# Two weight loads of the second feed-forward wait for the first w products of the gated delta rule

## The chip, the cores and the metric

One core of a Trainium2 chip. The metric is the device time of one execution in microseconds, the median of several runs. Times inside the kernel are counted from the start of the span of one profiled execution.

## What is computed

A decoder trunk of two layers on 256 tokens of width 1024, all in f32. Each layer adds a half feed-forward, a mixer and another half feed-forward:

```
for l in range(DEPTH):
    x = x + 0.5 * swiglu(rms_norm(x, norm_w[l, 0]), ...)
    h = rms_norm(x, norm_w[l, 1])
    x = x + (mixer_mla_gdn(h, ...) if l % 2 == 0 else mixer_spatial_gating(h, ...))
    x = x + 0.5 * swiglu(rms_norm(x, norm_w[l, 2]), ...)
```

The mixer of layer 0 has eight attention heads and eight heads of a gated delta rule. The latter works in chunks of 64 tokens: it solves a unit triangular system of 64 rows for each chunk and head, then goes through the four chunks in a recurrence:

```
sol = lax.linalg.triangular_solve(a, rhs, left_side=True, lower=True, unit_diagonal=True)
u, w = sol[..., :dv], sol[..., dv:]
def step(state, xs):
    v_new = u_i - w_i @ state
    o_i = qd_i @ state + a_i @ v_new
    state = state * exp(gl_i) + kt_i^T @ v_new
```

## The kernel before

**Weights in units.** All large weights are cut into units of at most 128x2048 elements (1 MB) and stream through a ring of four slots. For unit j, SyncE loads it into `raw` slot j % 4 (`load_unit`), ACT rounds it to `whi` (`hi`, L469), and VectorE subtracts to get `wlo` (`lo`, L892; for two units GpSimd does it, L439). TensorE multiplies with `whi` and `wlo`, which stands in for full f32. The load of unit j waits until the `wlo` of unit j - 4 is made, since that is the last reader of the `raw` slot: `lo_done(j - SLOTS)`.

**Order.** The kernel is written engine by engine; each engine's program is a fixed list, with semaphores between. SyncE's list is the loads in the order of use, then the stores of the result. A wait in it holds all loads behind it.

**Around the change.** Layer 0's mixer uses units `u_ab` to `u_ab + 15`; the last four are the output projection. The second feed-forward (of the same layer) uses the 33 units from `u_ffn[1]` on. Its first unit (gate) takes the slot of `u_ab + 12`, its second (up) that of `u_ab + 13`; the `wlo` of those two is made by GpSimd (`POOL_LO`) and counted by `pool_lo_ready`. Its third unit takes the slot of `u_ab + 14`, whose `wlo` VectorE makes after the recurrence.

**What TensorE does there.** After attention it builds the inverse of the triangular matrices by merging: five rounds (n = 0 to 4), each with the products m1, d and dt for two halves t of the tokens, by `quadrants` (L1710); ACT and VectorE move the sums out of PSUM between them. Then `AT_sums` (L1697), the w products (L1826), the transposes of q (L1835), the products u of the inverse with v (L1848), and the recurrence: for n = 0 to 3 the products with the state (L1861, L1865, not for n = 0), the state's update (L1873, not for n = 3) and the outputs (L1879). `w_sums` is counted up after the w products of t = 0 and again after those of t = 1; ACT copies w out then (L762). The output projection begins behind the recurrence (L1367).

A matmul of 64x64 in f32 leaves two matmul records and two weight-load records in the trace.

Of the kernel before, what the change touches and what calls it, by code (L numbers as in the profile page):

```python
# [73 lines left out]
def build_trunk(nc, x, positions, norm_w, w_gate, w_up, w_down, ab_in, q_norm, w_q_b, kv_norm, w_kv_b,  # L74
# [65 lines left out]
    for j, (_, _, pieces) in enumerate(units):  # L140
        per_slot[j % SLOTS] += len(pieces) if j else 0
        arrivals.append(per_slot[j % SLOTS])
# [4 lines left out]
    with ctx:  # L147
# [5 lines left out]
        def S(name):  # L153
            if name not in sems:
                sems[name] = ctx.enter_context(nc.semaphore(name))
            return sems[name]
# [126 lines left out]
        def unit_view(ring, j, kt, width):  # L283
            return ring[:, j % SLOTS, 0:kt * width].rearrange("p (k n) -> p k n", n=width)
# [10 lines left out]
        def lo_done(j):  # L295

            if j in POOL_LO:
                return S("pool_lo_ready"), POOL_LO.index(j) + 1
            return S("lo_ready"), j + 1 - sum(1 for i in POOL_LO if i < j)
# [16 lines left out]
        @block.sync  # L316
        def _(sp_):

            def load(dst, src, name):
                sp_.dma_start(dst, src).then_inc(S(name), 16)  # L320

            def load_first(i):
                load(unit_view(raw, 0, 8, 256)[:, 2 * i:2 * i + 2, :], units[0][2][0][1][:, 2 * i:2 * i + 2, :],
                     f"first_loaded{i}")

            for n in range(2):
                c = slice(512 * n, 512 * n + 512)
                for t in range(NT):
                    load(X[:, t, c], x[0, t * P:(t + 1) * P, c], f"x_loaded{t}{n}")
                load_first(n)  # L330
            for i in (2, 3):
                load_first(i)

            def load_unit(j):

                kt, width, pieces = units[j]
                if j >= SLOTS:
                    sp_.wait_ge(*lo_done(j - SLOTS))
                for c0, src in pieces:
                    dst = unit_view(raw, j, kt, width)[:, :, c0:c0 + src.shape[2]]  # L340
                    sp_.dma_start(dst, src).then_inc(S(f"raw_loaded{j % SLOTS}"), 16)

            def ffn_loads(base):
                for j in range(base, base + 33):
                    if j:
                        load_unit(j)
                    if j == 2:
                        load(C[:, P:n_const], const_dram[:, P:n_const], "const_loaded")

            ffn_loads(u_ffn[0])  # L350
            if stop_after == "ffn0":
                pass
            else:
                for j in range(u_ab, u_ab + 16):
                    load_unit(j)
            if stop_after not in ("ffn0", "ab"):
                ffn_loads(u_ffn[1])
                ffn_loads(u_ffn[2])
                for j in range(u_sg, u_sg + 24):
                    load_unit(j)  # L360
                ffn_loads(u_ffn[3])

            n_x = {"ffn0": 1, "ab": 2}.get(stop_after, 6)
            for q, (t, n) in enumerate(QUARTERS):
                sp_.wait_ge(S("x_updated"), 4 * (n_x - 1) + q + 1)
                sp_.dma_start(out[0, t * P:(t + 1) * P, 512 * n:512 * n + 512], X[:, t, 512 * n:512 * n + 512]
                              ).then_inc(S("out_stored"), 16)
            sp_.wait_ge(S("out_stored"), 64)
# [1596 lines left out]
```

## Time and profile before

| what | us |
|---|---|
| median of 3 runs | 1101.32 (1099.79 to 1102.14) |
| the profiled execution | 1101.23 |
| its span | 1099.3 |
| TensorE busy | 1066.0 (97% of the span) |
| TensorE weight loads busy | 971.4 (88%) |
| VectorE busy | 641.6 (58%) |
| ACT busy | 514.7 (47%) |
| GpSimd busy | 45.0 (4%) |

A chain of waits follows back from the last instruction, at each step to what released it. In its rows "issue" is time in which the engine waited for nothing that the profile shows. Windows show each engine's busy time in a stretch, with the granted TensorE clock as a share of full speed and the DMA engines' busy share. The DMA view lists the packets of each queue in a stretch; the queue of kind "instruction" brings instructions to an engine, the one called "hardware_dynamic" the loads that SyncE issues.

### The profile page before, as it was taken

What the parts mean: (1) busy time and instruction counts of PE and PEld (TensorE: products, weight loads), DVE (VectorE), ACT (ScalarE), POOL (GpSimd) and SP (SyncE); (2) the same over time, 40 slices, a digit from 0 to 9 for tenths busy, and PEclk for the clock granted to TensorE, in tenths of its full rate; (3) what the DMA queues carried; (4) which work ended last, traced back from release to release, by engine and by line L of the source; (5) the groups of instructions that cost most, each with busy time, mean ns of one, the idle gap of its engine ahead of it and who ended that gap; (6) DMA issues with size and microseconds to landing.
All of it is one profiled execution on the core that took longest, in us unless ns stands there. A gap on an engine that the chain in (4) does not pass through costs nothing.

```text
span 1099.3 us, 18954 instructions
## 1 busy us (share of the span) xinstructions
PE 1066.0 (97%) x8393; PEld 971.4 (88%) x8393; DVE 641.6 (58%) x779; ACT 514.7 (47%) x619; POOL 45.0 (4%) x34
## 2 busy tenths in 40 slices
PE   7999999998968999999999999999999999999998
PEld 6999988997757899999889999888788889999986
DVE  5755543699752775555348555545755547655532
ACT  6644433684653454444335444335565436444430
POOL 1000000112160000000000000000100000000000
PEclk9999999999999999999999999999999999999999
DMA  9855556253020466655547655555555475655531
GB/s 308 273 181 188 190 191 179 87 192 115 2 76 7 154 195 189 192 192 186 182 130 230 191 180 182 180 190 171 163 176 198 154 230 171 186 183 190 192 114 39
DMA packets 127194, 184.88 MB, mean 168 GB/s; under 512 B 4205, under 2 KB 101722, under 8 KB 126986
## 3 DMA queue, kind: packets, MB, share of 16 engines
q1 hardware_dynamic: 126368, 181.85, 50.9%
q0 software_dynamic: 448, 1.71, 0.5%
q8 instruction: 66, 1.08, 0.4%
q10 hardware_dynamic: 298, 0.12, 0.0%
q14 instruction: 14, 0.11, 0.0%
HBM read 182.62 MB, written 1.05 MB: 167 GB/s over the span
## 4 chain that ended last, share of the span: by engine, by line
PE 88%; DVE 5%; ACT 3%; issue 2%; DMA 1%; POOLq 0%; SPq 0%; POOL 0%; DVEq 0%; ACTq 0%
PE banks L1326 19%; PE banks L1327 19%; PE banks L1328 19%; PE banks L1367 7%; PE banks L1371 7%; PE banks L1368 7%; PE banks L1710 2%; DVE arena L1059 1%; PE banks L1436 1%; PE banks L1438 1%; PE banks L1437 1%; DVE wlo L892 1%; DMA raw<-in_ffn_w_up 1%; ACT whi L469 1%; PE banks L1400 1%
## 5 line engine op out<-in xcount | busy, mean ns | idle before, releaser
L892 DVE TENSOR_TENSOR wlo<-raw,whi 128x2048 fp32r<-128x2048 f32 (+1 forms) x169 | 386.7, 2294 | 228.5 <-ACT whi L469 228.4
L469 ACT ACTIVATE whi<-raw 128x2048 fp32r<-128x2048 f32 (+1 forms) x171 | 324.0, 1907 | 384.4 <-PE banks L1328 241.4
L1326 PE MATMUL banks<-xTh,whi 128*128 128x256 f32 x1408 | 396.8, 282 | 1.6 <-DVE wlo L1014 0.9
L1327 PE MATMUL banks<-xTl,whi 128*128 128x256 f32 x1408 | 395.8, 281 | 0.0
L1328 PE MATMUL banks<-xTh,wlo 128*128 128x256 f32 x1408 | 395.7, 281 | 0.0
L1326 PEld LDWEIGHTS banks<-xTh,whi 128*128 128x128 f32 x1408 | 265.5, 189 | 2.6 <-issue 1.2
L1327 PEld LDWEIGHTS banks<-xTl,whi 128*128 128x128 f32 x1408 | 265.6, 189 | 0.0
L1328 PEld LDWEIGHTS banks<-xTh,wlo 128*128 128x128 f32 x1408 | 265.5, 189 | 0.0
L1367 PE MATMUL banks<-whi,hTh 128*128 128x512 f32 x352 | 139.4, 396 | 0.0
L1368 PE MATMUL banks<-wlo,hTh 128*128 128x512 f32 x352 | 139.0, 395 | 0.0
L1371 PE MATMUL banks<-whi,hTl 128*128 128x512 f32 x352 | 110.6, 395 | 0.0
L1371 PEld LDWEIGHTS banks<-whi,hTl 128*128 128x128 f32 x352 | 66.0, 187 | 16.1
L1367 PEld LDWEIGHTS banks<-whi,hTh 128*128 128x128 f32 x352 | 66.0, 187 | 15.9
L1368 PEld LDWEIGHTS banks<-wlo,hTh 128*128 128x128 f32 x352 | 66.0, 187 | 15.8
L1326 PE MATMUL banks<-whi,xTh 128*128 128x512 f32 (+1 forms) x160 | 64.0, 400 | 0.0
L1327 PE MATMUL banks<-wlo,xTh 128*128 128x512 f32 (+1 forms) x160 | 62.7, 392 | 0.0
L1328 PE MATMUL banks<-whi,xTl 128*128 128x512 f32 (+1 forms) x160 | 62.6, 391 | 0.0
L927 DVE TENSOR_TENSOR arena<-banks,arena 128x512 f32<-128x512 f32 x44 | 30.4, 691 | 53.5 <-PE banks L1328 53.5
L918 DVE TENSOR_TENSOR arena<-banks,arena 128x512 f32<-128x512 f32 x44 | 30.4, 690 | 26.9 <-PE banks L1328 26.9
L1326 PE MATMUL banks<-whi,hTh 128*128 128x512 f32 (+1 forms) x108 | 43.6, 404 | 0.0
L1328 PE MATMUL banks<-whi,hTl 128*128 128x512 f32 (+1 forms) x108 | 42.2, 390 | 0.0
L1327 PE MATMUL banks<-wlo,hTh 128*128 128x512 f32 (+1 forms) x108 | 42.1, 390 | 0.0
(241 smaller groups left out, 976.6 us busy)
## 6 DMA issues: line engine op xcount, KB each, us to landing
raw<-in_ffn_w_up SPq DMA_DIRECT2D x44, 1024.0 KB, 5.4
raw<-in_ffn_w_down SPq DMA_DIRECT2D x44, 1024.0 KB, 4.9
raw<-in_ffn_w_gate SPq DMA_DIRECT2D x43, 1024.0 KB, 5.4
raw<-in_sg_w_in SPq DMA_DIRECT2D x16, 1024.0 KB, 5.5
raw<-in_ab_w_in SPq DMA_DIRECT2D x8, 1024.0 KB, 5.2
raw<-in_sg_w_out SPq DMA_DIRECT2D x8, 1024.0 KB, 5.3
raw<-in_ab_w_out SPq DMA_DIRECT2D x4, 1024.0 KB, 4.9
raw<-in_ab_w_in SPq DMA_DIRECT2D x2, 832.0 KB, 4.4
```

Of the source, the lines that this page charges most:

```text
L469: A(whi[:, j % SLOTS, 0:kt * width], raw[:, j % SLOTS, 0:kt * width], ACT.Copy).then_inc(S("hi_ready"), 1)
L892: TT(wlo[:, j % SLOTS, 0:n], raw[:, j % SLOTS, 0:n], whi[:, j % SLOTS, 0:n].bitcast(f32), ALU.subtract).then_inc(S("lo_ready"), 1)
L918: TT(gate[:, c % 2, :].rearrange("p (b n) -> p b n", n=SEQ), B[PAIR_BANK[c][0]][:].rearrange("p (b n) -> p b n", n=SEQ), bc(r_row.unsqueez ...
L927: TT(prod[:, c % 2, :], B[PAIR_BANK[c][1]][:], gate[:, c % 2, :], ALU.mult).then_inc(S("prod_ready"), 1)
L1059: ins = STT(y, src[:, 0:SEQ - back], w, y, ALU.mult, ALU.add)
L1326: mm(out_ap, lh, rh, start=first, stop=False)
L1327: mm(out_ap, lh, rl, start=False, stop=False)
L1328: return mm(out_ap, ll, rh, start=False, stop=last)
L1367: mm(o, hTh[:, kk, tok], wh[:, k, c], start=kk == 0, stop=False)
L1368: mm(o, hTh[:, kk, tok], wl[:, k, c], start=False, stop=False)
L1371: last = mm(o, hTl[:, kk, tok], wh[:, k, c], start=False, stop=False)
L1710: last = mm(banks[HC[r ^ s], pair[s], 64 * i:64 * i + 64], left, right, start=True, stop=True)
```

## The change

One line: SyncE waits until `w_sums` is at least 1 before it issues the loads of the second feed-forward.

```
@@ -354,6 +354,7 @@
                 for j in range(u_ab, u_ab + 16):
                     load_unit(j)
             if stop_after not in ("ffn0", "ab"):
+                sp_.wait_ge(S("w_sums"), 1)
                 ffn_loads(u_ffn[1])
                 ffn_loads(u_ffn[2])
                 for j in range(u_sg, u_sg + 24):
```

SyncE's list, where the output projection's four loads end and the second feed-forward's begin; `raw` is the ring, the brackets name the semaphores that a DMA waits for:

```order
 L341 DMA raw<-in_ab_w_out 128x2x1024 [waits lo_ready] x4
-L341 DMA raw<-in_ffn_w_gate 128x8x256 [waits pool_lo_ready]
+L341 DMA raw<-in_ffn_w_gate 128x8x256 [waits pool_lo_ready,w_sums]
 L341 DMA raw<-in_ffn_w_up 128x8x256 [waits pool_lo_ready]
 L341 DMA raw<-in_ffn_w_gate 128x8x256 [waits lo_ready]
```

The gate unit has a second semaphore to wait for; the up unit stands behind it and its own wait is unchanged.

TensorE's list from the w products to the second step of the recurrence, in the kernel before; `arena` holds the working matrices, `banks` is PSUM:

```order
1905 L1826 MATMUL banks<-arena 64x64 [waits dt_merged,kbe_ready]
1906 L1826 MATMUL banks<-arena 64x64 x15
1907 L1826 MATMUL banks<-arena 64x64 [waits dt_merged]
...
1911 L1848 MATMUL banks<-arena 64x64 [waits vb_ready,at_ready]
1912 L1848 MATMUL banks<-arena 64x64 x31
1913 L1873 MATMUL banks<-arena 64x64 [waits v_new_even,kt_ready,v_new_odd,qdT_out,w_ready]
1914 L1873 MATMUL banks<-arena 64x64 x7
1915 L1879 MATMUL banks<-arena 64x64 x8
1916 L1861 MATMUL banks<-arena 64x64 [waits state_ready]
```

Nothing moved on TensorE: its list after is the same. `w_sums` reaches 1 behind the row 1906; the two loads, which stood free of it, are now issued from there on.

## Rows read from the trace of the kernel before

**Rows 1.** Page: engines (busy, share, count), instruction queue (packets, MB), chain by engine.

```profile
PE 1066.0 (97%) x8393; PEld 971.4 (88%) x8393; DVE 641.6 (58%) x779; ACT 514.7 (47%) x619; POOL 45.0 (4%) x34
...
q8 instruction: 66, 1.08, 0.4%
...
PE 88%; DVE 5%; ACT 3%; issue 2%; DMA 1%; POOLq 0%; SPq 0%; POOL 0%; DVEq 0%; ACTq 0%
```

**Rows 2.** Timeline of SyncE's queue, 320 to 366 us: start, duration, line, tile.

```profile
320.99 0.37 SPq L341 DMA_DIRECT2D raw<-in_ffn_w_gate  x1
325.48 0.37 SPq L341 DMA_DIRECT2D raw<-in_ffn_w_up  x1
365.46 0.37 SPq L341 DMA_DIRECT2D raw<-in_ffn_w_gate  x1
```

**Rows 3.** Chain in order of time, 315 to 360 us: start, duration, what.

```profile
321.70 2.15 PE banks L1710 x125
323.85 4.50 issue
328.35 3.48 PE banks L1710 x95
331.82 0.60 issue
332.42 2.20 PE banks L1710 x127
334.62 1.25 issue
335.86 2.13 PE banks L1710 x124
337.99 1.51 issue
339.51 0.39 PE banks L1710 x10
...
343.14 0.51 PE banks L1697 x10
...
347.13 0.86 PE banks L1848 x21
...
350.06 0.06 PE banks L1861
...
352.60 0.06 PE banks L1861
```

**Rows 4.** DMA view, 321 to 325.75 us: all packets.

```profile
DMA packets 1035, 1.05 MB, mean 220 GB/s; under 512 B 13, under 2 KB 1035, under 8 KB 1035
```

**Rows 5.** DMA view, 325.75 to 326 us: instruction queue.

```profile
q8 instruction: 1, 0.02, 27.3%
```

**Rows 6.** DMA view, 344.5 to 344.75 us: instruction queue.

```profile
q8 instruction: 1, 0.02, 23.6%
```

**Rows 7.** Windows, TensorE: stretch, length, busy (count), clock, DMA share, GB/s.

```profile
308.00:310.00 2.00, 2.00 (x49) 0.50 0.00 0
...
328.00:330.00 2.00, 1.65 (x60) 0.51 1.08 375
330.00:332.00 2.00, 1.82 (x75) 0.64 0.04 12
```

**Rows 8.** Timeline of ACT: w copied out, and first feed-forward unit rounded.

```profile
344.25 1.22 ACT L762 ACTIVATE arena<-banks 128x256 f32<-128x256 f32 x4
...
365.27 1.95 ACT L469 ACTIVATE whi<-raw 128x2048 fp32r<-128x2048 f32 x1
```

**Rows 9.** DMA view, 324.75 to 325 us: the queue of SyncE's loads.

```profile
q1 hardware_dynamic: 96, 0.10, 110.4%
```

**Rows 10.** DMA view, 349.5 to 349.75 us: instruction queue.

```profile
q8 instruction: 1, 0.02, 32.4%
```

**Rows 11.** Timeline of TensorE, 302 to 308 us, idle before in brackets.

```profile
307.19 0.53 PE L1740 MATMUL banks<-C,arena 128*128 128x128 f32 x3 [2.64 <-ACT arena L698]
```

More of the change, by code:

```diff
@@ L356, in _ @@
             if stop_after not in ("ffn0", "ab"):
+                sp_.wait_ge(S("w_sums"), 1)
                 ffn_loads(u_ffn[1])
```

## The prediction

> **What bounds the kernel now.** Begin with the chain that ended last: TensorE holds 88% of it, everything else is small, 2% is "issue", time in which an engine waited for nothing that the profile shows [rows 1]. Time can come back only where TensorE stands still. The change moves two weight loads, so the next view is SyncE's issues around them: the gate unit at 320.99, the up unit at 325.48, and no further load before 365.46 [rows 2]. Only these two move. The third load after them waits for a `wlo` subtraction that VectorE does after the recurrence, as before.
>
> Third, the chain piece by piece over 320 to 353 us [rows 3]. Here TensorE runs the merges of the inverse, 64x64 matmuls, in pieces of some 127 records (a f32 matmul leaves two), and between pieces stands "issue": 4.50, 0.60, 1.25 and 1.51 us. These are no waits for ACT or VectorE. The page has a DMA queue of kind "instruction" with 66 packets and 1.08 MB [rows 1]: 16 KB a packet. A piece of 127 records is 127 weight loads and 127 matmuls, 254 instructions; the page counts 8393 of each, and 16786 over 66 packets are 254 again [rows 1]. So each piece is one packet, and "issue" is TensorE waiting for its next packet of instructions. With no load about, TensorE resumes at 332.42, 335.86, 339.51 and 343.14 [rows 3]. Those periods are 3.44, 3.65 and 3.63, mean 3.57 us, of which the matmuls fill 2.1 to 2.3; there the fetch is the bound.
>
> The 4.50 us stall stands under the first load. That load's 1035 packets are all that the DMA engines moved from 321 to 325.75 [rows 4]; the instruction packet comes only in the quarter us behind them [rows 5], at 325.79 in the answer's slices, and TensorE resumes 2.56 us later, at 328.35. In the quiet the packet of 344.74 [rows 6] comes 1.6 us after TensorE resumed at 343.14; here it came 4.1 us after 321.70. It waited for one load's share of its DMA engine. After the idle time the granted clock is 0.51 and then 0.64 on the mean of 2 us each [rows 7], which is the lower level, 1.2 GHz, for 2 x (0.49 + 0.36) x 2 = 3.4 us: the piece at 328.35 takes 3.48 us where others take 2.13 to 2.20.
>
> **What the merges give back.** From 321.70 to 332.42 are two pieces, 10.72 us. Without loads they should take two quiet periods, 2 x 3.57 = 7.14. Gain: 3.58 us. It is all on the path: the pieces before and after are TensorE or its fetch. The stall doesn't vanish to zero; what is late next is the ordinary fetch, and that is in the 3.57. Bounds from the rows: two periods of 3.44 give 3.84, two of 3.65 give 3.42.
>
> **What the wait adds.** SyncE has only the two loads and those behind them queued at this point; nothing else waits for SyncE. `w_sums` 1 is reached when half of the w products are made: ACT, which waits for the same count, starts at 344.25 [rows 8]. (All times stay on the clock of before; the shift of 3.6 us moves both sides alike.) GpSimd's subtractions, the other condition, were over when the up unit was issued at 325.48, so both loads are issued one behind the other at about 344.3 and 344.7. The first issue of before had its data moving from 322.0 and done by 325.8, 1.0 and 4.8 us after it. So load 1 moves from 345.3 to 349.05; load 2 follows without a gap, 64 packets of 1 KB on each of 16 engines, at 96 packets a quarter us over all engines, the rate in the middle of the first load [rows 9], 2.7 us, to about 351.8. Their data is wanted by ACT at 365.27 [rows 8]: 13 us of cover. If that cover went, each us late would cost a us; it does not go.
>
> **What the loads now lie over.** The recurrence: the v products and the first two of its steps, matmuls of the same small kind. It uses instructions slower, since it waits for VectorE in each step of some 2.5 us (350.06 to 352.60) [rows 3], and shows no fetch stall now. Fetches in it come at 344.74 [rows 6], for the boundary that is passed at 347.13, and at 349.59 [rows 10], for the next. That boundary: 21 records from 347.13, six batches of 16, and with the extra waits of the steps about 8 records of the third state product, which starts around 352.5 [rows 3]. Between packet and resuming stood 2.56 us in the merges, and at most 2.39 from 344.74 to 347.13; with 2.5, the packet at 349.59 lets TensorE go on at 352.1: 0.4 us to spare. But at 349.05 the fetch's engine has gone over to load 2. If the fetch waits for the share in progress, as it did for the first load, it comes at 351.8, TensorE resumes at 354.3, and 354.3 - 352.5 = 1.8 us is lost, on the path, since the steps are a chain. The bounds: nothing, if it slips in between the loads; 2.5 if load 2 is spread like a lone one.
>
> By the Trainium skill, "DMA: Bandwidth & Descriptors", section "Queues, rings and completion order", an engine changes rows after a packet of some 9 to 17 descriptors, at most 64. The 4.1 us above agree with the ceiling of 64, a whole share, not with the typical figure; by that figure nothing would be lost in the recurrence.
>
> **Sum.** -3.58 + 1.8 = -1.8 us. The profiled execution took 1101.23 us (span 1099.3), the median is 1101.32: the forecast is 1099.5 us, a change of 0.16%. A measurement of this kernel tells about 0.2%, 2.2 us, from no change.
>
> **Rivals.**
>
> The fetch slips in (gain whole). The request of the packet at 349.59 is made when the recurrence's first step is released at about 348.5, before load 1 ends at 349.05. If it is served in the change between the two loads, nothing is lost: 1101.3 - 3.6 = 1097.7. For it: the rows show a fetch behind one load, never behind two. Against: in the kernel before the packet came 1.1 us after that release, which is half a us too late for the change. The typical figure of the Trainium skill's DMA page would give this case too.
>
> The stall in the recurrence also costs the clock. After an idle of 2.64 us [rows 11] the clock was 0.50 [rows 7], after stalls of up to 1.51 us it stayed full. The new stall, 1.8 us, stands between. At the lower level for 3.4 us the dense merges lost 3.48 - 2.13 = 1.35 us; the same here gives -1.8 + 1.35 = -0.4: 1100.9.
>
> The loads hit one fetch earlier (the slower case). The fetch at 344.74 has 0.5 us before the first data at 345.3. Its place is fixed by count of instructions, the load's by `w_sums`. If it comes behind load 1 instead, at 349.1, TensorE resumes at 351.6 instead of 347.1: 4.5 lost, and the clock as in the merges 1.35, so -3.58 + 5.85 = +2.3: 1103.6. It decides from half a us of slip; both sides hang on TensorE's own place, which speaks against it.
>
> The change does nothing. The Trainium skill, "Runtime: NRT & Kernel Launch", section "Instruction fetch mechanics", has blocks of 16 KiB, as the packets here, and calls their cost mostly hidden; by it no load could slow TensorE through its fetch, and the time would stay. As a mechanism of this kernel: the 4.50 us would be something that comes at this point of the merges whatever is loaded. Against it stand the four stalls between pieces of equal length. Result 1101.3.
>
> **How the numbers follow.** Forecast with the stall in the recurrence, 0.46; whole gain 0.27; stall with the lower clock 0.13; no change 0.06; slower case 0.07; 0.01 left. The range holds the first four with their bounds: low 1101.3 - 3.84 - 0.7 for scatter = 1096.8, high 1101.7 (no change and 0.4, the scatter of the runs shown); outside are the slower case and tails. Faster than 1099.1: the whole gain (0.25) and that third of the forecast's spread in which the stall is under 1.3 us (0.15): 0.40. Slower 0.07. Within: 0.53. Both likely cases are gains; the question is only whether they pass 2.2 us.
>
> **What would show it.** In the chain after: periods of 3.4 to 3.7 us all through the merges, no clock under 1.00 there, w products begun 3.6 us sooner. Two loads issued half a us apart just at the w products. An "issue" of 1 to 2.5 us in the second or third step of the recurrence, behind an instruction packet that comes right after load 2. Wrong if the 4.50 us stays with no load about; if the recurrence shows no stall (then 1097.7); or if the stall stands in the v products (1103.6).

## The result: a gain in the merges, and more than that lost in the recurrence

The changed kernel takes 1104.02 us (median of 9 runs, 1100.52 to 1108.06), the kernel before 1101.32 (9 runs). The ratio is 1.0026, 95% interval 1.0015 to 1.0036: slower by a quarter of a percent. The forecast was 1099.5 within 1096.8 to 1101.7. A second set of 11 runs gave 1.0017 (1.0004 to 1.0029). The profiled execution of the changed kernel took 1104.02 us, its span is 1102.2.

Line numbers behind the added line are higher by one: L1711 is the merges' matmul, L1862 the state product, L1874 the state update, L1780 the transposes at which the output projection waits for VectorE.

The chain of the changed kernel in order of time, 312 to 372 us (start, duration, what):

```profile
322.43 2.15 PE banks L1711 x125
324.57 1.76 issue
326.33 2.18 PE banks L1711 x126
328.51 1.41 issue
329.92 2.20 PE banks L1711 x127
332.11 1.52 issue
...
340.64 0.51 PE banks L1698 x10
...
348.36 0.68 PE banks L1874 x16
...
350.12 1.97 issue
...
353.64 0.87 PE banks L1874 x16
...
357.69 1.94 PE banks L1880 x16
...
366.43 0.87 PE banks L1780 x8
```

The 4.50 us stall of [rows 3] is gone, the pieces run at 2.13 to 2.20 us, and from 322.43 to 340.64 the same work takes 18.21 us where it took 21.44: 3.23 us less. In the recurrence a new stall of 1.97 us stands within the third step's state product, and behind it everything takes longer: the state update 0.87 for 0.68, the last outputs 1.94 for 1.13 (the row of before reads 356.29 1.13).

SyncE's issues in the changed kernel, as [rows 2]:

```profile
341.75 0.37 SPq L341 DMA_DIRECT2D raw<-in_ffn_w_gate  x1
342.16 1.12 SPq L341 DMA_DIRECT2D raw<-in_ffn_w_up  x1
```

The DMA view from 349.25 to 349.5 us has the instruction packet among the last packets of the loads, and the one from 349.5 to 350.5 us shows that 14 packets were left:

```profile
q8 instruction: 1, 0.02, 26.2%
```

```profile
DMA packets 14, 0.01 MB, mean 11 GB/s; under 512 B 3, under 2 KB 14, under 8 KB 14
```

TensorE's windows in the changed kernel (stretch, length, busy and count, granted clock, DMA share, GB/s), as [rows 7]:

```profile
352.00:354.00 2.00, 1.90 (x35) 0.50 0.00 0
...
358.00:360.00 2.00, 2.00 (x17) 0.50 0.00 0
360.00:362.00 2.00, 2.00 (x6) 0.55 0.03 8
362.00:364.00 2.00, 2.00 (x11) 1.00 0.00 0
```

The clock is at its lower level from the end of the stall until near 361.8, some 10 us, where it had been full.

**The ledger.** The stretch from the second state update to the transposes measures what the stall costs: 351.15 to 363.29 in the kernel before, 12.14 us; 348.36 to 366.43 in the changed one, 18.07. Of the 5.93 us more, 1.97 are the stall; the 3.96 that are left are put down to the half clock: 3.04 of them up to the end of the last outputs, 0.92 in the projection behind them. The rest, at the marks above: +0.73 us up to 322.43 (the half clock after the idle of [rows 11] lasted longer in this execution; see the end), -3.23 in the merges, -0.29 from there to 348.36, +5.93, together +3.14 at the transposes; the span is 2.9 longer.

### The profile page after: what moved, and what is told of

Same layout as the page of the kernel before. It is cut to its first block, busy times and chain, and to the rows that moved or that the text cites. A ratio compares the mean times of both kernels' runs of the same rounds, so it can differ in the third digit from the quotient of the medians.

```text
span 1102.2 us, 18955 instructions
## 1 busy us (share of the span) xinstructions
PE 1072.3 (97%) x8393; PEld 977.4 (89%) x8393; DVE 641.6 (58%) x779; ACT 514.7 (47%) x619; POOL 45.4 (4%) x34
## 4 chain that ended last, share of the span: by engine, by line
PE 89%; DVE 5%; ACT 3%; issue 2%; DMA 1%; POOLq 0%; SPq 0%; POOL 0%; ACTq 0%; DVEq 0%
PE banks L1327 19%; PE banks L1329 19%; PE banks L1328 19%; PE banks L1368 8%; PE banks L1372 7%; PE banks L1369 7%; DVE arena L1060 1%; PE banks L1711 1%; PE banks L1437 1%; PE banks L1438 1%; PE banks L1439 1%; DVE wlo L893 1%; DMA raw<-in_ffn_w_up 1%; ACT whi L470 1%; PE banks L1401 1%
```

## Experiments

Theory from here on: the two loads cost time only by holding up a packet of TensorE's instructions; the stall that this makes is short, and the dear part is the half clock (the granted clock at 0.50) behind it. Rivals: the loads slow the recurrence or the clock in themselves; the later arrival of the data costs; the first profile was chance.

### The wait on the last outputs

```
-                sp_.wait_ge(S("w_sums"), 1)
+                sp_.wait_ge(S("o_sums"), 4)
```

> The same wait, but on the last outputs of the recurrence (o_sums 4): both loads are issued where TensorE begins the output projection with 512-column matmuls, which use few instructions per us. Theory (the loads cost time only by delaying TensorE's instruction packets; in the changed kernel that gave a 1.97 us stall in the recurrence, and the half clock behind it cost the rest): merges as in the changed kernel, no issue stall in the recurrence, clock 1.00 from the merges to the projection, loads landed before ACT wants them; time 1101.3 - 3.2 = 1098.1, ratio 0.997. Rival (the later landing or the longer wait itself costs): ratio 1.000 or more, with TensorE or ACT waiting on a load near 362 to 372 us. Rival (the recurrence is slowed by something else than the loads): the 2 us stall and the half clock stand in the recurrence as before.

Ratio 0.9964 (0.9952 to 0.9977), 1099.12 us. Because only 6 runs stood behind it, it was run again beside two later kernels:

> The kernel that waits for the last outputs once more, beside the two others of this job. Theory: ratio to before 0.9955 to 0.998, no issue stall and clock 1.00 from 325 us to the projection. Rival (its first figure of 0.9964 was luck of 6 runs): 0.999 or above.

Ratio 0.9985 (0.9976 to 0.9993), 1099.99 us: a smaller gain. The ratio lies just above the expected 0.9955 to 0.998 and below the rival's 0.999, and the interval reaches into both. Both intervals of this kernel lie below 1. The second profile's chain, with no issue of note in the recurrence:

```profile
349.43 0.68 PE banks L1874 x16
...
354.56 1.13 PE banks L1880 x16
...
361.56 1.09 PE banks L1780 x8
```

349.43 to 361.56 is 12.13 us, what the kernel before has. The loads were issued at 356.08 and 356.49 (first profile), ran from 357 to about 364 under the projection, and nobody waited for them. The gain of the merges stays in the main: from the resumption at 323.04 to that at 341.80 us the first profile has 18.76 us, the second 18.70 (323.02 to 341.72), where the kernel before has 21.44. So neither the wait nor the later arrival costs. This kernel is faster than the one before and, by intervals that do not meet, than the changed one. The expectation that the clock is full from 325 us on missed: in the second profile one piece of the merges ran at half clock:

```profile
325.17 2.03 issue
327.20 3.59 PE banks L1711 x126
...
331.00 2.19 PE banks L1711 x127
```

It cost next to nothing: 327.20 to 331.00 is 3.80 us, and the full-clock periods in the profiles of this kernel and of the changed one are 3.4 to 4.2 us. The issue of 1.4 us that follows a full-clock piece is used up by the slow one. This is why the half clock was cheap in the merges [rows 3, 7] and not in the recurrence.

### One load over the recurrence instead of two

```
+                if j == u_ffn[1] + 1:
+                    sp_.wait_ge(S("o_sums"), 4)
...
+                sp_.wait_ge(S("w_sums"), 1)
                 ffn_loads(u_ffn[1])
```

> Only the gate unit's load waits for w_sums 1, the up unit's waits for o_sums 4: one load lies over the recurrence instead of two. Theory (a packet of instructions waits for the share of the load in progress on its DMA engine; in the changed kernel it was the second load that held it): the load's data end about 3.8 us after they begin, near 346.6 us, before the packet's usual time of 346.8, so no stall beyond 0.3 us and the clock stays at 1.00: ratio 0.997. Rival (any load over the recurrence does it, by memory contention or by its placement): a stall of 1 us or more and the half clock remain, ratio 1.001 to 1.003.

Ratio 0.9983 (0.9972 to 0.9995), 1100.28 us. In the profile (span 1097.2) there is no stall in the recurrence and the clock there is 1.00, with the load's data moving at 248 GB/s under it:

```profile
344.00:348.00 4.00, 3.33 (x102) 1.00 0.75 248
```

So a load over the recurrence does not slow it by itself. The forecast of 0.997 lies just outside the interval; the runs spread over 4 us, and no profile shows whether some of them had a stall.

### Loads in pieces

Each of the two loads is issued as four DMAs of 256 KB, once where they stood before and once as in the change. (The counts that the readers wait for are raised to match, not shown.)

```
+                if j in CUT:
+                    for i in range(4):
+                        r = slice(2 * i, 2 * i + 2)
+                        sp_.dma_start(unit_view(raw, j, kt, width)[:, r, :], pieces[0][1][:, r, :]
+                                      ).then_inc(S(f"raw_loaded{j % SLOTS}"), 16)
+                    return
```

> The kernel before, with each of the two loads issued as four DMAs of 256 KB (two of the eight k-rows each). Nothing else moved. Theory A (the DMA engine turns to the instruction queue after the DMA in progress): the 4.50 us stall in the merges shrinks to about 4.50 - 3 x 0.7 = 2.4 us or less, and with it the half clock; ratio 0.997 to 0.999. Theory B (it turns to it only after all that was already handed to it): four DMAs issued one behind the other act as one, the stall stays at 4 to 4.5 us, ratio 1.000.

Ratio 0.9994 (0.9986 to 1.0003). The stall under the first load is 2.58 us, and a second of 2.44 comes under the other load:

```profile
325.47 2.58 issue
328.05 2.91 PE banks L1717 x126
330.96 2.44 issue
333.40 6.61 PE banks L1717 x235
340.01 0.49 issue
```

The stall is shorter than B asks and a little longer than A's 2.4, but the run doesn't tell A from B: TensorE came to this place 1.6 us later than in the kernel before (323.33 for 321.70), so its packet met the loads at another point. It does show the half clock again: 235 records took 6.61 us and 0.49 of issue, 7.10 for nearly two periods, about as fast as at full clock. The granted clock was 0.50 from 332 to 336 us.

> The changed kernel, with each of the two loads issued as four DMAs of 256 KB. Theory A of the run before (turn after the DMA in progress): the packet wanted near 347 us comes at most 0.7 us late, no stall in the recurrence beyond 0.3 us, clock 1.00: ratio 0.997. Theory B: the packet comes at the end of all eight, near 349.3 us, stall 1.5 to 2 us and half clock, ratio 1.001 to 1.004 as the changed kernel.

Ratio 1.0003 (0.9988 to 1.0019); inconclusive as a time. The 12 runs fall into two groups: four from 1098.55 to 1100.61 us with a mean granted clock of 0.994 to 0.997, and eight from 1102.73 to 1106.44 with 0.989 to 0.992. The profile (1105.09 us) is clear: a stall of 1.24 us and the half clock behind it, 349.84 to 367.41 or 17.57 us where 12.13 is normal.

```profile
349.84 0.68 PE banks L1881 x16
...
351.60 1.24 issue
...
367.41 0.87 PE banks L1787 x8
```

The instruction packet comes in the DMA view from 350.25 to 350.5 us, and 456 packets of the loads still follow from 350.5 to 353 us:

```profile
q8 instruction: 1, 0.02, 21.9%
```

```profile
DMA packets 456, 0.43 MB, mean 173 GB/s; under 512 B 33, under 2 KB 456, under 8 KB 456
```

It came 3.1 us behind the release of the first state update at 347.33, in the kernel before 0.9 us (348.65 to 349.59): 2.2 us late. A (at most 0.7 us) falls, and B (behind all eight) falls too.

### Stalls without any load

Here the loads wait for the last outputs, and VectorE does a reduction more ahead of the second state update; its result is used by nobody. The operand is X with 1024, 1536 or 2048 columns; the code is that of the 2048. TensorE's own idle time is shorter than the reduction, since it still computes outputs beside it: it is in the brackets of TensorE's rows below.

```
                 dve.wait_ge(S("s_sums"), n + 1)
+                if n == 1:
+                    link(nc.vector.tensor_reduce(rs_t[:, 31:32], X.rearrange("p t n -> p (t n)"), AX.X, ALU.max))
```

> The kernel of the run that waits for the last outputs (no load and no fetch stall in the recurrence), with one extra VectorE reduction of 128x1024 of X (its result is used by nobody) ahead of the second state update. TensorE then stands still about 1.1 us longer before the third step's state products, with no DMA about. It asks what an idle of that length costs by the clock. Theory (the half clock follows the idle time itself, whatever caused it, and decides between 1 and 2 us): clock stays 1.00, the time is that kernel's plus 1.1 us, ratio to before 0.9974. Rival (the half clock has another cause, the loads for one): the same here.

Ratio 0.9983 (0.9971 to 0.9996), 1099.93 us. The reduction took 1.23 us and left TensorE idle for 0.90, the clock stayed at 1.00, and the stretch is 13.39 us (352.20 to 365.59), 1.26 more than normal: the reduction and nothing else.

```profile
352.99 1.23 DVE small L1262
```

```profile
354.72 0.68 PE L1864 MATMUL banks<-arena 64*64 64x64 f32 x16 [0.90 <-DVE arena L1265]
```

The profiled execution is one of the four long ones of the 12 (1103.45 us; the other eight took 1099.09 to 1100.90). Its extra time lies ahead of the recurrence, where the granted clock was 0.58 from 316 to 320 and 0.56 from 320 to 324 us.

> As the run before, with a reduction of 128x2048: TensorE stands still about 2.2 us longer, as long as under the fetch stall of the changed kernel, but without loads and with its instructions there. Theory (idle time alone brings the half clock): windows from about 351 to 360 us show 0.50, and the time is the waiting kernel's plus 2.2 plus 2 to 4 us, ratio 1.000 to 1.002. Rival (it is the loads or the fetch that bring the half clock): clock 1.00, plus 2.2 us only, ratio 0.9984.

Ratio 1.0036 (1.0025 to 1.0047), 1106.16 us. The stretch is 349.77 to 369.29, 19.52 us: 7.39 more, of which 2.30 are the reduction and 5.1 are left for the clock. TensorE's idle time is 1.97 us.

```profile
350.56 2.30 DVE small L1262
...
369.29 0.87 PE banks L1782 x8
```

```profile
353.36 1.12 PE L1864 MATMUL banks<-arena 64*64 64x64 f32 x16 [1.97 <-DVE arena L1265]
```

The windows: half clock with no DMA about until 362 us, and up to near 366.

```profile
352.00:354.00 2.00, 0.64 (x12) 0.60 0.00 0
354.00:358.00 4.00, 4.00 (x72) 0.50 0.02 4
358.00:362.00 4.00, 3.84 (x42) 0.50 0.00 0
362.00:366.00 4.00, 4.00 (x11) 0.50 0.89 272
```

So idle time of that length, which is that of the changed kernel's stall, brings the half clock at this place with no load and no fetch in it. The theory holds; the size was above its upper bound of 1.002.

> As the 2.2 us stall in the recurrence, with a reduction of 128x1536, 1.75 us. No loads near. It asks where the clock turns. Theory (between 1.2 and 2.0 us of idle, by where it falls): some runs with half clock and some without, times spread over 5 us or more, ratio 0.999 to 1.003. Rival (a sharp bound at or above 2 us): all runs at that kernel's time plus 1.75, ratio 0.998, and a full clock in the profile.

Ratio 1.0025 (1.0010 to 1.0039), 1104.99 us, 6 runs from 1102.41 to 1106.06. The reduction took 1.76 us and left TensorE idle for 1.44; the stretch is 350.27 to 368.46, 18.19 us: 1.76 for the reduction and 4.30 left for the clock.

```profile
353.32 0.68 PE L1864 MATMUL banks<-arena 64*64 64x64 f32 x16 [1.44 <-DVE arena L1265]
```

The runs of the waiting kernel beside it are 1098.16 to 1101.79; with 1.76 added they would end at 1103.55, and four of the six lie above that. So the half clock comes in most runs; the two lowest, 1102.41 and 1103.39, may be runs without it. In the profiles of the recurrence TensorE kept the full clock behind an idle of 0.90 us and had the half clock behind every longer one: 1.24 (the loads in pieces), 1.44, 1.70 (the changed kernel again, below) and 1.97 us twice. Length alone is not the rule everywhere: in the merges the clock stayed full behind 1.76 us in several profiles, and 2.03 us of issue at the same place was followed by the half clock in the second profile of the waiting kernel and by the full one in this run's.

### The same reduction in the merges

```
                         dve.wait_ge(S("yt_sums"), 2 * (n - 1) + t + 1)
+                    if n == 2 and t == 0:
+                        link(nc.vector.tensor_reduce(rs_t[:, 31:32], X.rearrange("p t n -> p (t n)"), AX.X, ALU.max))
```

> The kernel that waits for the last outputs, with the extra reduction of 128x2048 (2.30 us) ahead of the third merge's m1 on VectorE, so that TensorE idles in the merges and not in the recurrence. Theory (the price of a stall is what its half clock meets: in the merges a piece of 127 records at half clock takes 3.3 us, no more than the 3.57 us that its next instructions take anyway, so the half clock is nearly free there): windows near 330 to 340 us show 0.50, pieces of 3.3 us with little issue between, and the time is that kernel's plus 1 to 2.5 us, where the same idle in the recurrence cost 7 to 8. Rival (a stall with half clock costs about the same wherever it stands): plus 6 us or more.

Ratio 0.9978 (0.9968 to 0.9988), 1099.01 us, against 0.9985 for the waiting kernel on the same chip: the 2.30 us of VectorE cost nothing. TensorE's timeline shows why:

```profile
323.01 2.15 PE L1713 MATMUL banks<-arena 64*64 64x64 f32 x127 [0.83 <-issue]
326.92 0.34 PE L1713 MATMUL banks<-arena 64*64 64x64 f32 x7 [1.76 <-issue]
327.42 1.98 PE L1713 MATMUL banks<-arena 64*64 64x64 f32 x119 [0.16 <-DVE arena L1232]
```

The reduction ran from 324.36 to 326.66 us, beside products that did not need it and then beside the 1.76 us in which TensorE waited for its next instructions anyway; the waiting kernel's first profile has the same 1.76 there. VectorE held TensorE up for 0.16 us. So the long idle that was expected never came, the clock stayed at 1.00, and the run does not test what such an idle costs in the merges. It shows that a late VectorE is free there. That half clock is cheap in the merges rests on the two profiles above, the second of the waiting kernel and that of the loads in pieces where they stood before.

### The changed kernel again

> The changed kernel once more, for a second profile and times on the same chip as the others. Theory: merges without the 4.50 us stall, a stall of 1.5 to 2.5 us in the recurrence, then half clock for 3 to 10 us; ratio 1.001 to 1.004. Rival (the first profile's half clock was chance): the stall, but full clock, ratio about 0.999.

Ratio 1.0017 (1.0004 to 1.0029), 1104.11 us. The stall is 1.70 us, the half clock lasts from near 352.8 to 363, the stretch is 18.37 us (348.13 to 366.50): 1.70 for the stall and 4.54 left for the clock. The instruction packet came between 349 and 349.25 us, with 22 packets of the loads left behind that. The first profile was no chance.

### The loads half way through the recurrence

```
-                sp_.wait_ge(S("w_sums"), 1)
+                sp_.wait_ge(S("v_sums"), 2)
```

> The wait on v_sums 2, one and a half steps into the recurrence: both loads move from about 348 to 354.6 us, past the fetch that the changed kernel hit and over the next one (before: 353.28, here 350.1). Theory (every fetch that falls under both loads comes at their end): its packet comes near 354.6 instead of 350.1, and TensorE stalls up to 3 us at the begin of the output projection, where the clock may fall too; ratio 0.998 to 1.002. Rival (only the recurrence is sensitive, the projection's long matmuls hide it): no stall, ratio 0.9965 as for the wait on the last outputs.

Ratio 0.9980 (0.9968 to 0.9991), 1100.06 us. The instruction packet comes between 358.25 and 358.5 us, with 342 packets of the loads still to come behind 358.5:

```profile
q8 instruction: 1, 0.02, 27.1%
```

```profile
DMA packets 342, 0.33 MB, mean 223 GB/s; under 512 B 15, under 2 KB 342, under 8 KB 342
```

Shifted by the 1.4 us that this execution was behind, its usual time is 354.7: it is 3.6 us late and still no stall shows, since the projection's 512-column matmuls take 0.23 us each and the piece in hand lasts. The rival holds in this profile: the projection hides a late packet, the recurrence doesn't. Its ratio of 0.9965 lies below the interval. That the packet comes at the end of both loads is wrong here.

## Why the prediction was wrong, point by point

**What bounds the merges**: right. The stalls fit fetches of instructions, and the 4.50 us one was the load's doing; it went with the load.

**The gain**: forecast 3.58 us, within 3.42 to 3.84. Measured over the same stretch, 3.23 in the first profile, below the lower bound, 3.50 in the second (322.48 to 340.42 us, 17.94), and 2.7 in both profiles of the waiting kernel. The quiet period of 3.57 was the mean of three; the first profile of the change has 3.90, 3.59, 3.71, 3.65 and 3.36, and the others reach 4.18.

**The new stall**: right in place, cause and size. Forecast 1.8 us within 0 to 2.5, at the third state product; measured 1.97 and 1.70. The loads were issued 0.41 us apart, as forecast, and the packet came at their end in both profiles. That part is not a rule, though: see what stays open.

**The step that failed** is the half clock behind it, twice. First its chance: I took a stall of 1.8 us to keep the full clock because stalls of 1.51 did so in the merges, put the term at nothing in the sum, and gave the other case 0.13. Both profiles of the change have the half clock, and idle times of 1.44 and 1.97 us without any load brought it too. Second its price: I put it at 1.35 us, the loss of one piece in the merges. It was 3.96 and 4.54 us here, 4.30 and 5.1 behind the reductions. The 1.35 is also not what the merges lost: the piece of 3.48 us was followed by only 0.60 of issue, so that its period was 4.07 us (328.35 to 332.42), 0.5 more than the 3.57. There the half clock could not show its cost, since the next instructions were late anyway, and it lasted 3.4 us instead of 10 or more. With a price of 4 that rival reads -3.58 + 1.8 + 4 = +2.2 us, 1103.5; measured is 1104.02.

**The slower rival** gave 1103.6, near the time, by a mechanism that did not happen: no fetch was hit at the v products.

**The others**: the fetch did not slip in. The changed kernel did do what it says. The Trainium skill, "Runtime: NRT & Kernel Launch", section "Instruction fetch mechanics", calls the cost of a block mostly hidden; for the 64x64 matmuls of the merges the runs show 1.2 to 2.1 us of every 3.4 to 4.2 in the open with no load beside them, and more under a load.

**What stays open.** When exactly an instruction packet gets its turn. In the kernel before and in both profiles of the change it came at the end of the loads, but in two runs within the second load, 2.2 and 3.6 us late; in the second of these the loads were whole too. A guess is that it waits for what has been handed to the DMA engine by the time of its request; no run tries that, and none shows how much of a load has been handed over at a given moment. "DMA: Bandwidth & Descriptors" of the Trainium skill has the engine change rows after at most 64 descriptors in "Queues, rings and completion order". In the run whose packet was 3.6 us late, 1277 packets went by on the 16 DMA engines from 354.7 to 358.25 us, some 80 on each; if a packet of the view is a descriptor, that is more than the ceiling, and the measurement decides. Also open is what decides between full and half clock behind an idle (full behind 1.76 us in the merges, half behind 1.24 us in the recurrence).

## What to carry to other kernels

A load is not free because its data are wanted late: where an engine runs through small instructions faster than they are fetched, as TensorE does in these merges, a large DMA beside it can delay the fetch by microseconds (2.2 to 3.6 here), so try to put such DMAs beside long instructions. Price a stall on TensorE by what follows it, too: in the recurrence a hold-up of 1.23 us that kept the full clock cost 1.3 us, while hold-ups of 1.24 to 1.97 us with the half clock behind them cost 5.4 to 6.2. And take the price of the lower clock from a stretch in which TensorE itself is the bound, not from one in which it waits anyway.

## What the runs showed of the hardware that was not expected

The lower clock lasted 3.4 us in one case, about 10 us in the changed kernel's profiles, and some 13.6 us behind the reduction of 2.30 us. The clock falls in every one of these kernels, too, behind the 2.64 us idle of [rows 11]. There the clock came back by 312 us in the profile of before, and in the changed kernel's it was still low after 316:

```profile
312.00:316.00 4.00, 3.85 (x80) 0.50 0.02 4
316.00:320.00 4.00, 4.00 (x167) 0.82 0.00 0
```

The runs of one kernel spread, too: the 34 of the kernel before on one chip go from 1099.84 to 1105.77 us. That the length of these stretches makes the spread is likely: the eleven fastest of the 34 have a mean granted clock of 0.992, the eleven slowest 0.989, which over 1100 us is some 6 us more at the lower level. Which stretches differ from run to run was not shown.
